# Row scaling before transposes, one stationary for four running sums, and one of 60 columns for the compressor, in a float32 network kernel

## The reference

```python
def ada_norm(x, g, shift, scale):
    return rms_norm_2(x, g) * (1 + scale[:, None, :]) + shift[:, None, :]

def rms_norm_2(x, g):
    y = xf * lax.rsqrt(jnp.mean(xf * xf, axis=-1, keepdims=True) + EPS)
    return (y * g.astype(jnp.float32)).astype(x.dtype)

# in the token mixer, native sparse attention: 15 windows of 32 tokens, 2 groups of heads
def compress(z, pos, w1, w2):
    zb = z[:, win_idx] + pos[None, None, :, None, :]
    zb = zb.transpose(0, 3, 1, 2, 4).reshape(B, G, n_c, CMP_LEN * D)   # 30 rows of 2048
    return jax.nn.gelu(zb @ w1) @ w2                                   # 2048 x 256, 256 x 64

# in the token mixer, forgetting attention: 4 heads
logf = jax.nn.log_sigmoid((f_logit + f_bias).astype(jnp.float32))
F = jnp.cumsum(logf, axis=1).transpose(0, 2, 1)
s = einsum(qb, kt) * scale + Fq[..., None] - F[:, :, None, :]
```

## Time and profile before

| What | us |
|---|---|
| runs: median (lowest to highest) | 1475.33 (1473.63 to 1478.91) |
| profiled execution: span | 1476.2 |
| PE busy (matmul) | 1442.5 |
| PE weight loads (PEld, beside PE) | 1241.8 |
| DVE busy | 1149.8 |
| ACT busy | 784.4 |
| POOL busy | 69.0 |

### The profile page before, as it was taken

How to read it: one execution, slowest core, us unless ns; L and a number is a source line. 1 busy time by engine, 2 the same in 40 slices (tenths; PEclk the granted TensorE clock), 3 DMA queues, 4 the chain that set the end, 5 groups by cost and what they waited for, 6 DMA issues and landing times. The chain is left out here.

```text
span 1476.2 us, 20955 instructions
## 1 busy us (share of the span) xinstructions
PE 1442.5 (98%) x8360; PEld 1241.8 (84%) x8360; DVE 1149.8 (78%) x1607; ACT 784.4 (53%) x1115; POOL 69.0 (5%) x91
## 2 busy tenths in 40 slices
PE   8998999999999999999999999999999999999997
PEld 6886889998888888788798888988888787888886
DVE  6797688888789877776778987789888676787643
ACT  7546554764555544656565453555535665555541
POOL 0021000000000000230000000000000500000000
PEclk9999999999999999999999999999999999999999
DMA  8132366998568777434347869578696332476450
GB/s 353 58 104 101 117 253 262 357 349 308 206 257 324 274 296 291 171 115 143 115 168 301 321 239 344 212 311 318 238 339 234 143 119 83 143 282 229 174 186 29
DMA packets 57153, 327.20 MB, mean 222 GB/s; under 512 B 6608, under 2 KB 7120, under 8 KB 27600
## 3 DMA queue, kind: packets, MB, share of 16 engines
q1 hardware_dynamic: 55440, 322.76, 58.5%
q10 hardware_dynamic: 1616, 3.10, 0.6%
HBM read 324.78 MB, written 1.05 MB: 221 GB/s over the span
## 5 line engine op out<-in xcount | busy, mean ns | idle before, releaser
L340 DVE TENSOR_TENSOR wlo<-raw,whi 128x2048 fp32r<-128x2048 f32 (+2 forms) x236 | 533.6, 2264 | 86.6 <-ACT whi L333 85.7
L333 ACT ACTIVATE whi<-raw 128x2048 fp32r<-128x2048 f32 (+2 forms) x236 | 445.8, 1895 | 135.4 <-PE ps L1615 96.5
L1367 PE MATMUL ps<-hreg_r,whi 128*128 128x512 f32 x1504 | 359.3, 391 | 0.4 <-DVE mix L1550 0.4
L1367 PEld LDWEIGHTS ps<-hreg_r,whi 128*128 128x128 f32 x1504 | 276.7, 188 | 54.3 <-DVE mix L1550 0.6
L381 DVE CUSTOM_DVE_ANT_0 adaw<-adaw,crow,colp 128x1024 f32<-128x1024 f32 x144 | 182.4, 1279 | 33.6 <-DMA adaw<-in_wada 33.3
L1376 PEld LDWEIGHTS ps<-hreg_r,wlo 128*128 128x128 f32 x1504 | 192.6, 191 | 7.0
L1376 PE MATMUL ps<-hreg_r,wlo 128*128 128x256 f32 x1504 | 195.6, 283 | 0.0
L1544 ACT ACTIVATE mix<-ps 128x512 f32<-128x512 f32 x93 | 55.5, 597 | 216.2 <-PE ps L1376 210.8
L1607 PE MATMUL ps<-whi,ireg_r 128*128 128x512 f32 x416 | 129.5, 392 | 1.7 <-ACT ireg_r L1501 1.7
L1615 PE MATMUL ps<-whi,ireg_r 128*128 128x512 f32 x416 | 128.4, 390 | 1.0 <-DVE ireg_r L1555 0.9
L1611 PE MATMUL ps<-wlo,ireg_r 128*128 128x512 f32 x416 | 128.3, 389 | 0.0
(11 more groups left out here) (422 smaller groups left out, 1958.0 us busy)
## 6 DMA issues: line engine op xcount, KB each, us to landing
raw<-in_wu SPq DMA_DIRECT2D x182, 1024.0 KB, 5.6
adaw<-in_wada SPq DMA_DIRECT2D x144, 512.0 KB, 5.0
raw<-in_wx SPq DMA_DIRECT2D x48, 1024.0 KB, 6.9
raw<-in_wu SPq DMA_DIRECT2D x4, 568.0 KB, 6.2
raw<-in_wu SPq DMA_DIRECT2D x2, 544.0 KB, 5.1
x<-in_x SPq DMA_DIRECT2D x2, 512.0 KB, 4.1
out<-hreg SPq DMA_DIRECT2D x2, 512.0 KB, 2.7
crow<-in_c ACTq DMA_DIRECT2D x1, 512.0 KB, 7.8
```

What stands on the lines that cost most here:

```text
L333: act.activation(self.whi[:, m, 0:width], self.raw[:, n % NRAW, 0:width], ACT.Copy).then_inc(*self.A.done("hi", n))
L340: dve.tensor_tensor(self.wlo[:, m, 0:width], self.raw[:, n % NRAW, 0:width], self.whi[:, m, 0:width].bitcast(F32), ALU.subtract).then_inc( ...
L1367: pe.matmul(self.ps[:, b, :], self.whi[:, m, c:c + 128], self.hboth[:, kt], start=kt == 0, stop=False)
```

## The change

1. **Norm.** DVE no longer writes the diagonal. It writes the scaled rows, `xn` = x times row factor, as two operations of 128 x 512, each with a signal of its own (`xs`). PE transposes the eight tiles of `xn` with the identity (one pass each), and waits for the second half of `xn` only ahead of the third pair.
2. **Running sums.** The log gates are written 32 times over for each head into `lfw`, 128 x 256 instead of 128 x 24, so that one stationary of 128 columns holds four heads; 2 products (4 passes) of 256 columns take the place of 8. `nF` is 128 x 256; head h's rows stand at partition 32 h. POOL does 8 steps on 128 x 256 with a constant `behind`, read from memory, that keeps each row's part.
3. **Compressor.** Upper and lower parts of the activations lie side by side in `aboth`, 60 columns. A slice takes two passes: 60 columns by `whi`, 30 columns by `wlo`; 16 passes in a unit instead of 24. `hidden` copies 60 x 256 out of PSUM without a table. HT becomes four float32 products with a constant `pair` that adds the two groups of 30 rows while it turns them (8 passes instead of 4). Gelu comes behind HT, on ACT (`gelu`), right behind `hidden(1)` and ahead of the exponentials of heads 7; it writes what DVE copied before. Some tiles have new places.

```diff
@@ -24,7 +24,7 @@
-CONSTS = [("ident", 128), ("mhalf", 32), ("ones", 256), ("mask", 128), ("triu", 512), ("iom4", 8), ("cmask", 32), ("bd", 8)]
+CONSTS = [("ident", 128), ("mhalf", 32), ("ones", 256), ("mask", 128), ("triu", 512), ("iom4", 8), ("cmask", 32), ("bd", 8), ("pair", 30), ("behind", 2)]
@@ -186,8 +186,8 @@
-        self.ahi = ir[:, at:at + 960].rearrange("p (a b c) -> p a b c", a=2, b=16)
-        self.alo = hr[:, 5120:6080].rearrange("p (a b c) -> p a b c", a=2, b=16)
+        self.aboth = hr[:, 4096:6016].rearrange("p (a b c) -> p a b c", a=2, b=16)
+        self.ahi, self.alo = self.aboth[:, :, :, 0:30], self.aboth[:, :, :, 30:60]
@@ -197,7 +197,7 @@
-        self.part, self.oneb = narrow[0:3, 0:256], narrow[0:3, 256:384]
+        self.part, self.oneb = narrow[:, 0:256], narrow[:, 256:384]
@@ -219,14 +219,13 @@
-        self.dgt = self.rs[:, 512:1024].rearrange("p (a b) -> p a b", b=128)
-        self.nFb = sb("nFb", [128, 1024], mybir.dt.bfloat16)[0:3, :].rearrange("p (a b) -> p a b", a=4)
+        self.nFb = sb("nFb", [128, 256], mybir.dt.bfloat16)[:, :]
@@ -427,8 +428,10 @@
             .then_inc(*self.V.done("ms", st, t))
         dve.wait_ge(*self.G("rs", st, t))
         if st not in (M0, "end"):
-            dve.tensor_scalar(self.dgt[:, t, :], self.ident, s[:, 2 + t:3 + t], float(D) ** 0.5, ALU.mult, ALU.mult)\
-                .then_inc(*self.V.done("dg", st, t))
+            for c in range(2):
+                cols = slice(512 * c, 512 * c + 512)
+                dve.tensor_scalar(self.xn[:, t, cols], self.x[:, t, cols], s[:, 2 + t:3 + t], float(D) ** 0.5, ALU.mult, ALU.mult)\
+                    .then_inc(*self.V.done("xs", st, t, c))
         else:
             self.step(dve, self.V)(dve.tensor_scalar(s[:, 2 + t:3 + t], s[:, 2 + t:3 + t], float(D) ** 0.5, None, ALU.mult), "rstd", st, t)
@@ -442,13 +445,14 @@
 
     def norm_pe(self, pe, st, t):
 
-        pe.wait_ge(*self.V("dg", st, t))
         for kp in range(4):
+            if kp % 2 == 0:
+                pe.wait_ge(*self.V("xs", st, t, kp // 2))
             for k in range(2):
                 kt = 2 * kp + k
-                mm = pe.matmul(self.ps[:, 4 * (1 - t) + kp, 128 * k:128 * k + 128], self.x[:, t, kt * 128:kt * 128 + 128],
-                               self.dgt[:, t, :], start=True, stop=True)
-            mm.then_inc(*self.P.done("T", st, t, kp))
+                tr = pe.transpose(self.ps[:, 4 * (1 - t) + kp, 128 * k:128 * k + 128], self.xn[:, t, kt * 128:kt * 128 + 128],
+                                  self.ident)
+            tr.then_inc(*self.P.done("T", st, t, kp))
 
     def halves(self, kp, t):
         return slice(2 * kp, 2 * kp + 2), slice(128 * t, 128 * t + 128)
@@ -2327,17 +2331,16 @@
-        v["ZZ"], v["A"], v["DU"] = sc(16, [128, 4, 256]), sc(20, [128, 2, 16, 30]), sc(20, [128, 2, 4, 2, 64])
-        v["hg"], v["PC"] = sc(16, [30, 2, 256]), sc(16, [128, 2, 128])
-        v["HTv"], v["Sc"] = sc(18, [128, 2, 2, 4, 16]), sc(19, [128, 2, 2, 4, 16])
+        v["ZZ"], v["A"], v["DU"] = sc(16, [128, 4, 256]), self.att(0, [128, 2, 16, 30]), sc(20, [128, 2, 4, 2, 64])
+        v["hb"], v["PC"] = self.att(1, [60, 2, 256]), sc(16, [128, 2, 128])
+        v["HTv"], v["Sc"] = self.att(0, [128, 2, 2, 4, 16]), sc(19, [128, 2, 2, 4, 16])
-        v["lf3"] = self.frt(80, [128, 2, 4, 3])
-        v["nF"] = self.gf[0:3, 1792:2816].rearrange("p (a b) -> p a b", a=4)
-        v["behind"] = self.gf[0:3, 3008:3009]
+        v["lfw"] = self.frt(640, [128, 2, 4, 32])
+        v["nF"] = self.gf[:, 1792:2048]
@@ -2389,13 +2392,15 @@
                 pe.wait_ge(*free)
                 pe.wait_ge(*A("Ah", st))
                 pe.wait_ge(*V("Al", st))
-            o = ps[0:30, 6 + kv, 0:256]
+            both, upper = ps[0:60, 6 + kv, 0:256], ps[0:30, 6 + kv, 0:256]
             for k in range(8):
                 kt = 8 * half + k
                 wh, wl = self.whi[:, m, 256 * k:256 * k + 256], self.wlo[:, m, 256 * k:256 * k + 256]
-                pe.matmul(o, self.ahi[:, kv, kt, :], wh, start=kt == 0, stop=False)
-                pe.matmul(o, self.alo[:, kv, kt, :], wh, start=False, stop=False)
-                mm = pe.matmul(o, self.ahi[:, kv, kt, :], wl, start=False, stop=kt == 15)
+                if kt < 15:
+                    pe.matmul(both, self.aboth[:, kv, kt, :], wh, start=kt == 0, stop=False)
+                mm = pe.matmul(upper, self.ahi[:, kv, kt, :], wl, start=False, stop=False)
+                if kt == 15:
+                    mm = pe.matmul(both, self.aboth[:, kv, kt, :], wh, start=False, stop=True)
             mm.then_inc(*P.done("unit", n))
 
         def out(c, kts, t, free=None):
@@ -2466,8 +2471,9 @@
-                        pe.matmul(ps[:, 2 * r + i, 128 * qt:128 + 256 * qt], self.oneb,
-                                  self.nFb[:, 2 * (g - 8) + i, 0:128 + 128 * qt], start=False, stop=False)
+                        h = 32 * (2 * (g - 8) + i)
+                        pe.matmul(ps[:, 2 * r + i, 128 * qt:128 + 256 * qt], self.oneb[h:h + 3],
+                                  self.nFb[h:h + 3, 0:128 + 128 * qt], start=False, stop=False)
@@ -2521,10 +2527,8 @@
         chunk("C", 0, 0, A("pj", st, "B"))
         pe.wait_ge(*V("lf", st))
         pe.wait_ge(*A("gbc", st, 1))
-        for h in range(4):
-            o = ps[0:3, 4 + h // 2, 256 * (h % 2):256 * (h % 2) + 256]
-            for t in range(2):
-                mm = pe.matmul(o, v["lf3"][:, t, h, :], self.triu[:, t, :], start=t == 0, stop=t == 1)
+        for t in range(2):
+            mm = pe.matmul(ps[:, 4, 0:256], v["lfw"][:, t].rearrange("p h r -> p (h r)"), self.triu[:, t, :], start=t == 0, stop=t == 1)
         mm.then_inc(*P.done("F", st))
         chunk("C", 0, 1, V("pj", st, "B"))
         pe.wait_ge(*V("rope", st, 284))
@@ -2582,20 +2586,20 @@
         scores(6)
         compress(1, 1)
         turned_probs(5)
-        chunk("E", 0, 0, A("hg", st, 0))
+        chunk("E", 0, 0, A("hb", st, 0))
         values(5)
         pe.wait_ge(*A("turn", st, "D", 1))
-        pe.wait_ge(*A("hg", st, 1))
+        pe.wait_ge(*A("hb", st, 1))
         for kv in range(2):
             for k in range(2):
                 c = 256 * kv + 128 * k
-                tr = pe.transpose(ps[:, 5, c:c + 30], v["hg"][:, kv, 128 * k:128 * k + 128], ident[0:30, 0:30])
-        tr.then_inc(*P.done("HT", st))
+                mm = pe.matmul(ps[:, 5, c:c + 30], v["hb"][:, kv, 128 * k:128 * k + 128], self.pair, start=True, stop=True)
+        mm.then_inc(*P.done("HT", st))
 
         scores(7)
-        chunk("E", 0, 1, A("hg", st, 1))
+        chunk("E", 0, 1, A("hb", st, 1))
         turned_probs(6)
-        pe.wait_ge(*V("HT", st))
+        pe.wait_ge(*A("HT", st))
         pe.wait_ge(self.s_cw2, 16)
         for k in range(2):
             pe.matmul(ps[:, 5, 0:30], self.cw2k[:, l, k, :], v["HTk"][:, k, :], start=k == 0, stop=k == 1)
@@ -2676,18 +2680,15 @@
     def mixer_pool(self, pool, l):
 
 
-        st, v = ("m", l), self.mixer_tiles()
+        st, row = ("m", l), self.mixer_tiles()["nF"]
         step = self.step(pool, self.G)
         pool.wait_ge(*self.V("nF", st))
         step(pool.memset(self.oneb, 1.0))
-        step(pool.tensor_tensor(v["behind"], self.ident[0:3, 1:2], self.ident[0:3, 2:3], ALU.add))
-        for h in range(4):
-            row = v["nF"][:, h, :]
-            for keep in (v["behind"], self.ident[0:3, 2:3]):
-                step(pool.tensor_copy(self.part, row))
-                step(pool.tensor_tensor(self.part, self.part, keep.to_broadcast([3, 256]), ALU.mult))
-                step(pool.tensor_tensor(row, row, self.part, ALU.subtract))
-            step(pool.tensor_copy(self.nFb[:, h, :], row), "nFb", st)
+        for k in range(2):
+            step(pool.tensor_copy(self.part, row))
+            step(pool.tensor_tensor(self.part, self.part, self.behind[:, k:k + 1].to_broadcast([128, 256]), ALU.mult))
+            step(pool.tensor_tensor(row, row, self.part, ALU.subtract))
+        step(pool.tensor_copy(self.nFb, row), "nFb", st)
 
     def mixer_act(self, act, l):
         P, A, V = self.P, self.A, self.V
@@ -2724,7 +2725,17 @@
 
         def hidden(kv):
             act.wait_ge(*P("unit", UNIT[("cw1", l), kv, 1]))
-            act.activation(v["hg"][:, kv, :], ps[0:30, 6 + kv, 0:256], ACT.Gelu_apprx_tanh).then_inc(*A.done("hg", st, kv))
+            act.activation(v["hb"][:, kv, :], ps[0:60, 6 + kv, 0:256], ACT.Copy).then_inc(*A.done("hb", st, kv))
+
+        def gelu():
+            ht = ps[:, 5, :].rearrange("p (v k c) -> p v k c", v=2, k=2)
+            act.wait_ge(*P("HT", st))
+            act.wait_ge(*V("pads", st))
+            act.activation(v["HTk"], ht[:, 0, :, 0:30], ACT.Gelu_apprx_tanh)
+            for k in range(2):
+                src = ht[:, 1, k, 0:30].rearrange("p (g c) -> p g c", g=2).unsqueeze(2).to_broadcast([128, 2, 4, 15])
+                ins = act.activation(v["HTv"][:, k, :, :, 0:15], src, ACT.Gelu_apprx_tanh)
```

(20 more changed lines are left out.)

## The result

| | us |
|---|---|
| kernel before: median of 4 runs (lowest to highest) | 1475.19 (1473.63 to 1478.91) |
| changed kernel: median of 4 runs | 1465.58 (1464.26 to 1466.45) |
| ratio, with its 95% interval | 0.9931 (0.9914 to 0.9948) |
| span of the profiled execution, before and changed | 1476.2 and 1462.3 |

The change makes the kernel 9.6 us faster (0.7%; by the interval 7.7 to 12.7). The spans of the two profiled executions lie 13.9 us apart. That is not the effect. A run takes somewhat longer than its span: 2.0 us in the changed kernel (the execution with a span of 1462.3 took 1464.26), and 1.8 us in every other run of the kernel before whose span is on record. So the profiled execution of before took some 1478.0 us, which is among the slower ones of its kernel. The traces must be compared stage by stage, and against more than one trace of before.

What follows compares the result with a forecast made beforehand. PE, busy 1442.5 of 1476.2 us, bounds the kernel, with DVE next in line. Norms -0.5, running sums -5.3 and compressor -3.5 sum to -9.3: span 1466.9, forecast 1466.0 us after 0.9 for the profiled span; range 1456 to 1471.

Steps and rivals of the forecast that it cites:

- scaling of 512 columns: Norms, DVE: 0.48 us per operation from SBUF rows; the pair takes 0.80, so DVE 0.6 us more at each of 14.
- m0: Norms of m0: DVE runs without slack to the rotation PE awaits, so its extra work arrives: +0.6 each half, +1.2 us.
- f01, f10, f11: Norms there: DVE's idle time absorbs t = 0; only the last piece, factor to first product, gains: -0.3 each, -0.9 us.
- running sums: Both mixers: 16 passes become 4, ScalarE's gate row covers DVE's wider write: -2.65 us each, -5.3 in all.
- compressor to HT, each layer: 24 passes become 16: -3.65 us, less 1.35 waiting for `wlo` and 0.5 longer HT: -1.8 net a layer.
- Gelu behind HT: ACT in each layer: chunk E and values of heads 6, some 8 us of PE, cover the later Gelu: 0.
- The central step: All stages: PE's removed passes shorten the span only where DVE and ACT, which prepare its next input, keep up.
- Rival D: Boundaries: PE's granted clock falls to 0.50, costing 3.3 us a fall, slower from four falls on; chance 0.05.
- Rival A: Whole kernel: every pass counts, as ACT and DVE run earlier too: -25.2 us, 1450 us; chance 0.14.
- B: Norms: scaling runs one column a cycle, 0.72 us each: +3.6 us, 1469.6; chance 0.09.
- C: Late Gelu: ACT's table load and three activations hold the exponentials, 1 to 1.5 us a layer, 1468.5; chance 0.03.
- E: Compressor: passes with 60 stationary columns cost twice: +4.6 us, 1470.6; chance 0.03.

Runs made afterwards that it cites:

- part 1 alone: Kernel before with only the norm change (scaled rows in two operations, eight transposes for sixteen product passes); ratio 1.0005, median 1476.37 us of 12 runs.
- part 3 alone: Kernel before with only the compressor change, `rs` 32 columns narrower to make room for the constant; 1470.63 us, one run.

## Why the prediction was right, and where it was not

The forecast was 1466.0 us and a difference of 9.3; measured are 1465.58 and 9.6. Point by point, with the changed kernel's first trace against one or both of before (the one without a disturbance in the stretch):

| Term | forecast, us | measured, us |
|---|---|---|
| scaling of 512 columns | 0.48, pair 0.80 | 0.483, pair 0.79 |
| norms of MOE | -1.5 | -0.76 and -0.97 |
| f00 | +0.1 | +0.2 to +0.4; with the clock's fall +1.4 to +1.6 |
| m0 | +1.2 | +0.3; +1.2 to +1.6 in part 1 alone |
| m1 | +0.6 | +0.6 |
| f01, f10, f11 | -0.9 | -0.3, 0.0, -0.3; -0.3 each in the second trace |
| running sums | -2.65 twice | -2.75, -2.71 |
| compressor to HT, each layer | -1.8 net | -2.16, then +0.4 |
| Gelu behind HT | 0 | no wait of PE for it |

**The central step held:** the price of a pass times the passes is not the gain, since DVE, a chain of DVE, ScalarE and POOL, or `wlo` ends last. Of 25 us of passes 9.6 arrive. The norms come to -1.1 us in the first trace of the changed kernel and to 0 in the second, with the clock's fall, for a forecast of -0.5; that the total came so near is in part luck, since m0 was taken 0.9 us too dear and the clock's fall at nothing.

**The scaling operation** was rightly taken from the two SBUF rows and not from the PSUM row: 483 ns against an estimate of 480. By the Trainium skill, "VectorE: DVE Perf Modes", section on the TRN2 errata, the estimate was 0.33 us; the measurement decides for the rows, whose fixed part is larger.

**The compressor** came out as worked: a wait of 1.27 us for `wlo` (forecast 1.35), and HT takes 0.91 us from its start to the products behind it, against 0.33, 0.6 longer (forecast 0.5, a guess for which no row was given):

```profile
672.27 0.96 PE L2596 MATMUL ps<-cst,ireg 60*128 60x30 f32 x7
...
673.18 0.90 PE L2469 MATMUL ps<-ireg 64*128 64x128 f32 x7
```

The net of -1.8 a layer is what the traces show, 1.75. Behind HT the changed kernel loses 0.4 us up to the next norm, and part 3 alone 0.6, no more than HT itself grew: so PE waited for no exponentials behind Gelu.

**The running sums** were forecast from ScalarE's gate row as the last to be ready, with DVE's wider `lfw` under its cover. The timelines of DVE and ACT of the changed kernel bear this out:

```profile
603.74 0.43 DVE L2940 TENSOR_TENSOR ireg<-ireg 128x256 f32<-128x256 f32 x1 [1.66 <-ACT ireg L2752]
```

```profile
605.10 1.07 ACT L2269 ACTIVATE greg<-ps 128x512 f32<-128x512 f32 x2
```

`lfw` is done at 604.17, the gate row at 606.17, and PE starts at 606.31, 0.14 us later; in the trace of before the gate row ends at 611.16 and PE starts at 611.31, 0.15 later. The rotation that the profile names ends at 606.28, later than the gate row, but PE's stream doesn't wait for it there: it waits for `lf` and `gbc` alone. That the gate row is the last is read from the code and this equal distance. The write takes 0.43 us where the narrow one took 0.18, the quarter of a us forecast, and it costs nothing.

**Failed: m0.** The step "what DVE does more arrives there: +0.6 for each half, +1.2" took the row that ends at 606.60 for a chain without slack from the first diagonal on. DVE and PE at the first norm of m0, before, changed, and with part 1 alone:

```profile
580.16 0.29 DVE L430 TENSOR_SCALAR rs<-cst,st 128x128 f32<-128x128 f32 x1 [0.66 <-POOL st L441]
580.75 1.95 PE L449 MATMUL ps<-rs,x 128*128 128x128 f32 x16
```

```profile
573.61 0.88 DVE L433 TENSOR_SCALAR hreg<-x,st 128x512 f32<-128x512 f32 x2 [0.66 <-POOL st L444]
575.83 1.03 PE L453 MATMUL ps<-cst,hreg 128*128 128x128 f32 x8
```

```profile
578.78 0.88 DVE L432 TENSOR_SCALAR hreg<-x,st 128x512 f32<-128x512 f32 x2 [0.67 <-POOL st L443]
579.33 1.09 PE L452 MATMUL ps<-cst,hreg 128*128 128x128 f32 x8 [0.93 <-DVE hreg L432]
```

In the first trace of before DVE begins the diagonal 0.6 us ahead of PE's norm; in the second it is 0.96 ahead, and the second norm of m0 comes 0.4 us sooner behind the first (10.46 us for 10.85). So at that lead DVE's lateness did reach PE. In the changed kernel DVE is 2.2 us ahead, 1.7 in its second trace, the stretch takes 10.34 to 10.45 us, and the 0.6 of t = 0 does not arrive. Of the 0.6 of t = 1 0.4 arrives (20.14 us from the second norm to the running sums, for 19.71). In part 1 alone DVE is late: it begins 0.55 us ahead of a norm for which PE has by then waited 0.93. From the first norm to the running sums that trace is 1.2 us longer than the first of before, which has about the same lead, and 1.6 longer than the second; at like lead, then, all of the step's 1.2 arrives. So the step was right for the lead that the one trace showed, and the lead of DVE over PE is not fixed. Why DVE leads more in the changed kernel was not tried.

**As forecast: f01, f10, f11.** Forecast 0.3 each: 0.3 at f01 and f11 in both traces of the changed kernel, at f10 nothing in the first and 0.3 in the second and in part 1 alone. The stretches at f10 scatter by up to 1.2 us in traces of either form of the norm, so one trace tells little there. PE waits there 0.94 us for the scaled rows and 0.40 for the upper part, both new, as forecast.

**Missed: the clock at f00.** Rival D had a chance of 0.05 and was set at 3.3 us a fall; against it stood that the boundaries ran at 1.00. At f00 it happened in the traces of part 1 alone and in the changed kernel's second, and not in its first nor in the one with the compressor's split moved up: two of four executions that have the transposes and the 2 us wait. It never did in the traces with the diagonal there, nor in those with the transposes and without the wait. It costs 1.2 to 1.3 us. The Trainium skill, "TensorE: Matmul & The Clock Gate", Part 4, says that transposes do not count as busy in the way products do; what these traces show is that transposes and a wait of 2 us together can be followed by the lower clock, and that transposes alone were not. No trace has products and a wait of 2 us at f00, so whether the transposes have a part in it, or the wait does it by itself, stays open.

**Wrong in the bookkeeping:** "the profiled span lies 0.9 us above the median of the runs" set a span beside times. A time of the kernel before is 1.8 us more than its span, so its profiled execution was 2.7 us above the median. The forecast stands on the difference of 9.3 us, which this doesn't touch, but the sum was made on a disturbed trace: the experts' stage in it was 3.3 us longer than in the second trace, and 2.4 us more of it were waits of PE (3.3 for 0.9).

Rival A's 1450 us, B's 0.72 us scaling, C's late Gelu and E's double passes are each excluded by a measurement above.

## What to carry to other kernels

Halving the passes of the busiest engine is worth what the engines that feed it can follow: read, at each place, which operation of another engine ends last before the product, and whether the edit adds to that one. A pass that moves its price from a 98% engine to the next one in line gains only where the next one has a gap; here 13 us of passes brought about 1 by the traces, and nothing that the runs could tell. And when a wait shows in one place, look whose order makes it: moving one split at one boundary and one in the mixer brought 3.5 us by the traces, more than all fourteen norms, while a like move at three other boundaries cost 15 us, because what was moved was needed first.

## What the runs showed of the hardware

- In the compressor a pass of 256 moving columns over fp32r weights starts every 0.118 us, with 60 and with 30 stationary columns alternating, as it did with 30 alone, so the wider stationary was free here. The plain float32 passes of the running sums take longer, and are no slower with more columns either: four with 128 stationary columns take 0.75 us (606.31 to the next line at 607.06), 0.19 each, against 0.22 with 3 columns.
- With the splits moved behind, PE waits 5.1 us at each of three boundaries; the granted clock falls to 0.50 while it waits and stands there for 6.8 us in all (at f01 from 740.4 to 747.2, PE working again from 743.33). About 1 us goes on the first eight passes (2.08 us for 1.12).
- How long the clock stays low differs between executions of the same code. Around 172 us it was 6.8 us in the first trace of before and 3.4 in the second, 3.4 in the first trace of the changed kernel and not at all in its second. At f00 the two falls lasted 3.4 us and cost 1.2 to 1.3.
- Executions of the kernel before scatter by 5 to 10 us within a comparison (1471.87 to 1481.83 over all), those of the changed kernel by 2 to 3.5. The traces place part of it in the experts' stage (3.3 us) and in how long the clock stays low around 172 us (1.6 us between the two traces of before).
